# Transposing the probabilities of two attention units together in a three-layer transformer kernel

## The chip, the cores and the metric

The kernel runs on one core of a Trainium2 chip. What counts is the device time of one execution in microseconds (us). The engines are TensorE (PE in the profile; its weight loads are PEld), VectorE (DVE), ScalarE (ACT), GpSimd (POOL) and SyncE (SP), each with its own stream of instructions. They wait for one another by semaphores.

## The reference, cut to what matters

A sequence of 256 tokens of width 1024 goes through an attention layer with two kinds of attention (a windowed one with grouped keys and a sink, here A; a neighbourhood one, here B), an MLP, a retention layer, a second MLP, and then a hybrid layer with three attentions: M (causal), D (causal, over the 256 best keys by an index score) and X (over a memory). All in float32. What the change touches is the softmax in the middle of A, B, M and D:

```python
s = jnp.einsum('bqhd,brkhd->bhqrk', qr, kr).astype(jnp.float32) * scale
s = jnp.where(col_valid[:, None, :], s + bias, -jnp.inf)
p = jax.nn.softmax(s.reshape(B, B_HEADS, GRID_W, kh * GRID_W), axis=-1)
...
return jnp.einsum('bhqrk,brkhd->bqhd', p, vr)
```

## The kernel before

All products with weights are done as three matmuls of split numbers: a weight half tile (128x1024) is copied to `whi` by ScalarE (L969) and the rest, raw minus `whi`, goes to `wlo` on VectorE (L1433). TensorE then streams matmuls over these halves (L415 to L417, L504, L469 to L472). The halves are prepared four or five ahead of TensorE.

Each attention has 8 units of two heads and one block of 128 queries. The units are spread over steps `s`, and each step also holds one half tile of the next projection (`n_half`, `t_half`), so that TensorE has a stream of projection matmuls between two pieces of attention. The sequence "AB" runs A's 8 units and then B's (16 units, 18 steps and one more), "M" and "D" have 8 units each. Every engine has its own program that walks through the same steps, and its order is the order in the code; nothing reorders it later. For unit i the chain is:

- TensorE: `att_scores` (L596), both units of a pair in the even step
- VectorE: `att_scored` (scale and bias, L1545 for A, L1556 otherwise), `att_peaked` (row maxima, L1565 or L1570)
- ScalarE: `att_exp` (L1052), two activations with their sums
- VectorE: `att_summed` (reciprocal, L1585)
- ScalarE: `att_scaled` (L1062), two activations
- TensorE: `att_transposed` (L608), four 128x128 transposes, two where only 128 keys count
- `att_copied`: out of PSUM, on VectorE for an even unit (L1580) and on ScalarE for an odd one (L1074)
- TensorE: `att_values` (L628), both units of a pair, four steps after the scores of the even one

PSUM has 8 banks, `ps0` to `ps7`. `take` in the program of TensorE draws the next bank from a ring and waits until the engine that reads the previous contents is done; `give` puts a bank back as soon as its matmuls are issued:

```python
b = ring.popleft()
if b in held:
    w.wait_ge(*at("free", held[b]))
held[b] = name
```

So which bank a tile gets, and whose reading it waits for, follows from the order of all `take` and `give` calls. Beside the attention, some steps have work of their own: in step 3 of AB ScalarE squares the kb projection (`hn_squares`, L987) and VectorE sums these squares (`hn_sums`, L1457); VectorE applies rotary factors with `roped` (L1662, L1664), which frees the two banks of a projection and, for Dk, may start only when TensorE has transposed the same half of Dq (`rp_transposed`, L578).

## Time and profile before

| | |
|---|---|
| Median of 3 runs | 984.32 us (984.25 to 984.86) |
| The profiled execution | 984.95 us, its span 983.1 us |
| TensorE busy | 973.8 us, 99% of the span |
| VectorE, ScalarE, GpSimd busy | 687.2, 536.1 and 154.8 us |
| Share of TensorE in the chain that ended last | 95% |
| Granted clock over the span | 0.999 |
| AB, M and D, from first scores to last values | about 39 to 117, 753 to 791 and 809 to 848 us |

Read it from the busiest engine. TensorE has work nearly all the time, and the profile's chain of work that ended last is almost wholly its own; idle time of another engine costs nothing by itself.

### The profile page before, as it was taken

How to read it: one execution, taken by the hardware profiler on the slowest of the kernel's cores; microseconds unless marked ns; L12 is line 12 of the kernel's file. 1: busy time of each engine (PE TensorE's matmuls, PEld its weight loads, DVE VectorE, ACT ScalarE, POOL GpSimd, SP SyncE). 2: the span in 40 equal slices, each digit the busy share in tenths (PEclk: the TensorE clock that was granted, in tenths of full speed). 3: DMA queues.
4: the chain of work that ended last, by engine and by line, in shares of the span. 5: the costliest groups of instructions: out<-in, count | busy, mean ns of one | idle time of the engine just before them, and what ended most of it. 6: DMA issues, size and time to landing. Idle time of an engine off the chain costs nothing.

```text
span 983.1 us, 14468 instructions
## 1 busy us (share of the span) xinstructions
PE 973.8 (99%) x5608; PEld 838.5 (85%) x5608; DVE 687.2 (70%) x1036; ACT 536.1 (55%) x900; POOL 154.8 (16%) x193
## 2 busy tenths in 40 slices
PE   9999999999999999999999999999999999999997
PEld 7788788888888888888888888888887789999995
DVE  6797766766666667786567566657678997667674
ACT  6678755444556553454455455444546756655452
POOL 2732017920001002310010000000550100000001
PEclk9999999999999999999999999999999999999999
DMA  9875645575564654445547655664644454545531
GB/s 339 294 184 191 194 145 180 192 222 180 172 203 153 216 200 140 139 147 177 195 146 220 206 172 176 202 220 142 215 142 155 133 171 130 170 131 167 177 129 43
DMA packets 110307, 174.76 MB, mean 178 GB/s; under 512 B 4256, under 2 KB 72992, under 8 KB 110240
## 3 DMA queue, kind: packets, MB, share of 16 engines
q1 hardware_dynamic: 109664, 173.27, 54.0%
q8 instruction: 45, 0.74, 0.3%
q10 hardware_dynamic: 576, 0.57, 0.2%
q14 instruction: 22, 0.18, 0.1%
HBM read 172.78 MB, written 1.05 MB: 177 GB/s over the span
## 4 chain that ended last, share of the span: by engine, by line
PE 95%; ACT 1%; POOL 1%; DMA 1%; DVE 1%; issue 0%; SPq 0%; POOLq 0%; ACTq 0%; DVEq 0%
PE ps L504 24%; PE ps L472 15%; PE ps L415 12%; PE ps L417 12%; PE ps L416 12%; PE ps L470 9%; PE ps L469 2%; PE ps L596 2%; PE ps L608 2%; PE ps L628 1%; DMA raw<-in_w_in_e 1%; PE ps L556 1%; ACT whi L969 0%; PE ps L578 0%; PE ps L646 0%
## 5 line engine op out<-in xcount | busy, mean ns | idle before, releaser
L1433 DVE TENSOR_TENSOR wlo<-raw,whi 128x1024 fp32r<-128x1024 f32 x313 | 376.2, 1239 | 25.1 <-ACT whi L969 12.0
L969 ACT ACTIVATE whi<-raw 128x1024 fp32r<-128x1024 f32 x313 | 315.7, 1048 | 41.9 <-PE ps L504 26.0
L472 PE MATMUL ps<-hT,whi 128*128 128x512 f32 x644 | 229.7, 396 | 0.0
L470 PE MATMUL ps<-hT,wlo 128*128 128x256 f32 x736 | 190.3, 279 | 0.0
L470 PEld LDWEIGHTS ps<-hT,wlo 128*128 128x128 f32 x736 | 138.8, 189 | 7.6
L472 PEld LDWEIGHTS ps<-hT,whi 128*128 128x128 f32 x644 | 120.9, 188 | 25.0
L415 PE MATMUL ps<-whi,hT 128*128 128x512 f32 (+1 forms) x312 | 122.6, 393 | 0.1
L417 PE MATMUL ps<-whi,hT 128*128 128x512 f32 (+1 forms) x312 | 120.1, 385 | 0.0
L416 PE MATMUL ps<-wlo,hT 128*128 128x512 f32 (+1 forms) x312 | 119.9, 384 | 0.0
L1773 DVE TENSOR_TENSOR arena<-ps,arena 128x256 f32<-128x256 f32 x80 | 33.4, 422 | 101.1 <-ACT arena L1182 101.0
L504 PE MATMUL ps<-whi,urh 128*128 128x512 f32 x328 | 101.5, 390 | 0.0
L504 PE MATMUL ps<-wlo,urh 128*128 128x512 f32 x328 | 101.3, 389 | 0.0
L504 PE MATMUL ps<-whi,url 128*128 128x512 f32 x328 | 101.3, 389 | 0.0
L1182 ACT ACTIVATE arena<-ps 128x256 f32<-128x256 f32 x80 | 30.2, 385 | 129.5 <-PE ps L472 129.5
L504 PEld LDWEIGHTS ps<-wlo,urh 128*128 128x128 f32 x328 | 61.6, 188 | 12.9
L504 PEld LDWEIGHTS ps<-whi,url 128*128 128x128 f32 x328 | 61.6, 188 | 12.8
L504 PEld LDWEIGHTS ps<-whi,urh 128*128 128x128 f32 x328 | 61.4, 188 | 11.6
L417 PEld LDWEIGHTS ps<-whi,hT 128*128 128x128 f32 x312 | 58.6, 188 | 11.9
L415 PEld LDWEIGHTS ps<-whi,hT 128*128 128x128 f32 x312 | 58.7, 188 | 11.8 <-ACT whi L969 0.5
L416 PEld LDWEIGHTS ps<-wlo,hT 128*128 128x128 f32 x312 | 58.7, 188 | 10.5
L415 PE MATMUL ps<-hT,whi 128*128 128x256 f32 (+1 forms) x232 | 66.8, 288 | 0.0
L416 PE MATMUL ps<-hT,whi 128*128 128x256 f32 (+1 forms) x232 | 65.6, 283 | 0.0
(216 smaller groups left out, 1495.3 us busy)
## 6 DMA issues: line engine op xcount, KB each, us to landing
raw<-in_w SPq DMA_DIRECT2D x64, 1024.0 KB, 5.9
raw<-in_w_in SPq DMA_DIRECT2D x34, 1024.0 KB, 5.2
raw<-in_w_in_o SPq DMA_DIRECT2D x24, 1024.0 KB, 5.3
raw<-in_w_out_o SPq DMA_DIRECT2D x8, 1024.0 KB, 5.0
raw<-in_w_in_e SPq DMA_DIRECT2D x7, 1024.0 KB, 11.1
raw<-in_w_mem SPq DMA_DIRECT2D x4, 1024.0 KB, 10.7
raw<-in_w_out_e SPq DMA_DIRECT2D x4, 1024.0 KB, 5.0
raw<-in_w_out SPq DMA_DIRECT2D x4, 1024.0 KB, 4.9
```

Of the source, the lines that this page charges most:

```text
L415: e.matmul(o, a[0], b[0], start=start, stop=False)
L416: e.matmul(o, a[0], b[1], start=False, stop=False)
L417: return e.matmul(o, a[1], b[0], start=False, stop=stop)
L469: e.matmul(o, h[:, k, :], both, start=True, stop=False)
L470: mm = e.matmul(o[:, 0:256], l[:, k, :], hT[0][:, k, :], start=False, stop=False)
L472: mm = e.matmul(o, h[:, k, :], both, start=False, stop=k == 7)
L504: mm = e.matmul(bank("acc", stage, 2 * tb + i), x[p], t[p % 2][:, 0, 512 * i:512 * i + 512], start=start and p == 0, stop=stop and p == 2)
L596: mm = e.matmul(b[:, j * 256:j * 256 + nk], q_of(h, qb), k_of(h, nk), start=True, stop=True)
L969: e.activation(split_half(i)[0], raw_half(i), ACT.Copy).then_inc(*up("hi", ("hi", i)))
L1182: e.activation(dst, bank("mm", label, m)[:, 256:512], ACT.Copy).then_inc(*up("aev", ("lc", label, m)))
L1433: e.tensor_tensor(l, raw_half(i), h.bitcast(F32), ALU.subtract).then_inc(*up("lo", ("lo", i)))
L1773: e.tensor_tensor(d, bank("mm", label, m)[:, 0:256], d, ALU.add).then_inc(*up("dev", ("t", label, m), ("free", ("mm", label, m))))
```

## The change

In TensorE's program the transposes of an odd unit no longer stand in the odd step, between two pieces of projection, but in the even step, directly behind those of the even unit. The other two programs are ordered for it: VectorE does both maxima of a pair (`att_scored`, `att_peaked`, twice) at the head of the even step, and copies the even unit's transposed probabilities after them instead of before; ScalarE does in the odd step first the exponentials and then both scalings (they used to stand one before the exponentials and one behind the weights), and copies the odd unit's transposed probabilities in the even step. No instruction is added or removed. X is left as it is.

```diff
--- before.py
+++ after.py
@@ -657,8 +657,9 @@
                 if s % 2 == 0 and s < n:
                     att_scores(*SEQ[key][s])
                     att_scores(*SEQ[key][s + 1])
-                if 0 <= s - 2 < n:
+                if s % 2 == 0 and 0 <= s - 2 < n:
                     att_transposed(*SEQ[key][s - 2])
+                    att_transposed(*SEQ[key][s - 1])
 
             def index_scores(u):
                 qb, hs = IX8[u]
@@ -1076,23 +1077,19 @@
 
             def att_step(key, s):
                 n = len(SEQ[key])
-                if 0 <= s - 2 < n:
-                    att_copied(*SEQ[key][s - 2])
+                if s < n:
+                    att_exp(*SEQ[key][s])
+                if key == "AB" and s == 3:
+                    hn_stored("qb")
                 if key == "AB" and s == 7:
                     v_stored("vb", 0, 512, bvv[:, 1, :], "E")
                 if s % 2 and s < n:
                     att_scaled(*SEQ[key][s - 1])
+                    att_scaled(*SEQ[key][s])
+                if s % 2 == 0 and 0 <= s - 2 < n:
+                    att_copied(*SEQ[key][s - 1])
                 if key == "AB" and s in (8, 9):
                     row_squares("mem", osb, osb, [(S["m"], 16), (S["m"], 16)], (s - 8,))
-                if key == "AB" and s == 3:
-                    hn_stored("qb")
-                if s < n:
-                    att_exp(*SEQ[key][s])
-
-            def att_ends(key, s):
-
-                if s % 2 and s < len(SEQ[key]):
-                    att_scaled(*SEQ[key][s])
 
             def gate_low(label, c):
 
@@ -1171,7 +1168,6 @@
                     v_stored("xv", 0, 512, xv[:, 1, :], "mem")
                 if s in (10, 14):
                     oe_high((10, 14).index(s) + 1)
-                att_ends("AB", s)
             used(("oe", 1), 1)
             oe_high(3)
             used(("oe", 3), 1)
@@ -1324,7 +1320,6 @@
                     used(("Dq", "Dk")[s // 4], s % 4)
                 else:
                     used("Dv", s - 8)
-                att_ends("M", s)
                 if s == 7:
                     y_high(0, 0)
             y_high(0, 1)
@@ -1357,8 +1352,6 @@
                     used(("xq", s // 2), s % 2)
                 else:
                     merge_half(0, s - 4)
-                if s < 10:
-                    att_ends("D", s)
                 if s in (7, 11):
                     y_high(1, s // 11)
             for s in range(16):
@@ -1586,14 +1579,13 @@
 
             def att_step(key, s):
                 n = len(SEQ[key])
-                if 0 <= s - 2 < n:
+                if s % 2 == 0 and s < n:
+                    att_scored(*SEQ[key][s])
+                    att_peaked(*SEQ[key][s])
+                    att_scored(*SEQ[key][s + 1])
+                    att_peaked(*SEQ[key][s + 1])
+                if s % 2 == 0 and 0 <= s - 2 < n:
                     att_copied(*SEQ[key][s - 2])
-                if s < n:
-                    if s % 2 == 0:
-                        att_scored(*SEQ[key][s])
-                    att_peaked(*SEQ[key][s])
-                    if s % 2 == 0:
-                        att_scored(*SEQ[key][s + 1])
 
             def att_ends(key, s):
                 if s < len(SEQ[key]):
@@ -1735,16 +1727,16 @@
                 if s == 7:
                     v_stored("vb", bvv[:, 0, :], "E")
                 att_step("AB", s)
+                weights_to(first_half["kb"] + LO_ROW[s])
+                att_ends("AB", s)
                 if s == 1:
                     hn_scaled("qb")
+                if s == 3:
+                    hn_sums("kb")
+                if s == 5:
+                    hn_scaled("kb")
                 if s in (4, 5, 6):
                     memory_low(range(3 * s - 12, min(3 * s - 9, 8)))
-                weights_to(first_half["kb"] + LO_ROW[s])
-                if s == 5:
-                    hn_scaled("kb")
-                att_ends("AB", s)
-                if s == 3:
-                    hn_sums("kb")
                 if s == 14:
                     v_stored("xv", xv[:, 0, :], "mem")
                 if s in (8, 10, 14):
```


The first place is TensorE in step 4 of AB and the start of step 5 (`ps3` and `ps4` take the scores of units 4 and 5). Before, where "..." stands for the matmuls of half a vb tile:

```order
L596 MATMUL ps3<-arena 128x256 [waits s_aev]
L596 MATMUL ps3<-arena 128x256
L596 MATMUL ps4<-arena 128x256 [waits s_aev]
L596 MATMUL ps4<-arena 128x256
L608 MATMUL ps5<-cst,arena 128x128 x4
L415 MATMUL ps0<-whi3,hT 128x512 [waits s_lo,s_hi]
...
L417 MATMUL ps1<-whi3,hT 128x512
L608 MATMUL ps3<-cst,arena 128x128 [waits s_aev,s_dev]
L608 MATMUL ps3<-cst,arena 128x128 x3
L415 MATMUL ps0<-whi4,hT 128x512 [waits s_lo,s_hi]
```


After:

```order
L596 MATMUL ps3<-arena 128x256 x2
L596 MATMUL ps4<-arena 128x256 [waits s_aev]
L596 MATMUL ps4<-arena 128x256
L608 MATMUL ps5<-cst,arena 128x128 [waits s_aev]
L608 MATMUL ps5<-cst,arena 128x128 x3
L608 MATMUL ps3<-cst,arena 128x128 [waits s_aev,s_dev]
L608 MATMUL ps3<-cst,arena 128x128 x3
L415 MATMUL ps0<-whi3,hT 128x512 [waits s_lo,s_hi]
```


The four transposes of unit 3 have moved up by a half tile of matmuls. They write bank `ps3` in both, but this bank now holds scores that were made four rows earlier, and the row waits for VectorE (`s_dev`) to have read them.

The second place is TensorE in step 8 of M, from the values of units 4 and 5 to the first matmuls of the Dv projection. Before:

```order
L628 MATMUL ps4<-arena 64x128 [waits s_aev,s_dev]
L628 MATMUL ps4<-arena 64x128 x3
L608 MATMUL ps2<-cst,arena 128x128 [waits s_aev,s_dev]
L608 MATMUL ps2<-cst,arena 128x128 x3
L578 MATMUL ps3<-cst,arena 128x128 [waits s_po]
L578 MATMUL ps3<-cst,arena 128x128 x3
L578 MATMUL ps0<-cst,arena 128x128 [waits s_po]
L578 MATMUL ps0<-cst,arena 128x128 x3
L415 MATMUL ps7<-whi0,hT 128x512 [waits s_lo,s_hi]
```


After:

```order
L628 MATMUL ps4<-arena 64x128 [waits s_aev,s_dev]
L628 MATMUL ps4<-arena 64x128 x3
L608 MATMUL ps7<-cst,arena 128x128 [waits s_aev,s_dev]
L608 MATMUL ps7<-cst,arena 128x128 x3
L608 MATMUL ps3<-cst,arena 128x128 [waits s_aev]
L608 MATMUL ps3<-cst,arena 128x128 x3
L578 MATMUL ps6<-cst,arena 128x128 [waits s_po]
L578 MATMUL ps6<-cst,arena 128x128 x3
L578 MATMUL ps5<-cst,arena 128x128 [waits s_po]
L578 MATMUL ps5<-cst,arena 128x128 x3
L415 MATMUL ps1<-whi0,hT 128x512 [waits s_lo,s_hi,s_dev]
```


With the transposes of unit 7 ahead of those of Dq (L578), one more bank has been taken when the Dv projection takes its two, and its first matmul now also waits for VectorE (`s_dev`). The bank is that of Dk's first half, which `roped` frees.

The third place is ScalarE in steps 2 and 3 of AB: exponentials of a unit are two L1052 rows (L1053 after), scalings two L1062 rows (L1063), the weight copy L969 (L970), the copy of unit 1 L1074 (L1075), the stored qb L994 (L995), the squares of kb L987 (L988). Before:

```order
L1052 ACTIVATE arena,stat<-arena,stat 128x257 [waits s_dst]
L1052 ACTIVATE arena,stat<-arena,stat 128x257
L969 ACTIVATE whi<-raw 128x1024 [waits s_wd]
L1074 ACTIVATE arena<-ps 128x512 [waits s_tp]
L1062 ACTIVATE arena<-arena,stat 128x256 [waits s_dst]
L1062 ACTIVATE arena<-arena,stat 128x256
L994 ACTIVATE arena<-ps,gain 128x4x128 x2
L1052 ACTIVATE arena,stat<-arena,stat 128x257 [waits s_dst]
L1052 ACTIVATE arena,stat<-arena,stat 128x257
L987 ACTIVATE arena<-ps 128x512 [waits s_mm] x2
L1062 ACTIVATE arena<-arena,stat 128x256 [waits s_dst]
```


After:

```order
L1053 ACTIVATE arena,stat<-arena,stat 128x257 [waits s_dst]
L1053 ACTIVATE arena,stat<-arena,stat 128x257
L1075 ACTIVATE arena<-ps 128x512 [waits s_tp]
L970 ACTIVATE whi<-raw 128x1024 [waits s_wd]
L1053 ACTIVATE arena,stat<-arena,stat 128x257 [waits s_dst]
L1053 ACTIVATE arena,stat<-arena,stat 128x257
L995 ACTIVATE arena<-ps,gain 128x4x128 [waits s_tp] x2
L1063 ACTIVATE arena<-arena,stat 128x256 [waits s_dst]
L1063 ACTIVATE arena<-arena,stat 128x256
L1063 ACTIVATE arena<-arena,stat 128x256 [waits s_dst]
L1063 ACTIVATE arena<-arena,stat 128x256
L988 ACTIVATE arena<-ps 128x512 [waits s_mm] x2
```


Both scalings of the pair now stand directly ahead of the squares of kb; before, one of them stood behind these.

## Rows read from the trace of the kernel before

**Rows 1.** The page's busy time of TensorE and its granted clock by slices.
```profile
PE 973.8 (99%) x5608; PEld 838.5 (85%) x5608; DVE 687.2 (70%) x1036; ACT 536.1 (55%) x900; POOL 154.8 (16%) x193
...
PEclk9999999999999999999999999999999999999999
```

**Rows 2.** The waits of TensorE, longest first: the first of four rows.
```profile
PE ps L700 <- DVE arena L1709: 1.2, 1, 1.2
```

**Rows 3.** Timeline of TensorE: streams of matmuls and transposes between them.
```profile
43.20 0.39 PE L415 MATMUL ps<-whi,hT 128*128 128x512 f32 x1
...
45.69 0.39 PE L417 MATMUL ps<-whi,hT 128*128 128x512 f32 x1
...
50.34 1.03 PE L568 MATMUL ps<-cst,arena 128*128 128x128 f32 x8
51.21 0.60 PE L608 MATMUL ps<-cst,arena 128*128 128x128 f32 x4
...
59.61 0.39 PE L417 MATMUL ps<-whi,hT 128*128 128x512 f32 x1
...
60.20 0.48 PE L415 MATMUL ps<-whi,hT 128*128 128x512 f32 x1
...
62.83 0.39 PE L417 MATMUL ps<-whi,hT 128*128 128x512 f32 x1
```

**Rows 4.** Timeline around step 4 of AB: TensorE, ScalarE, VectorE.
```profile
56.58 0.66 PE L608 MATMUL ps<-cst,arena 128*128 128x128 f32 x4
...
50.63 0.51 ACT L1052 ACTIVATE arena<-arena,stat 128x257 f32<-128x257 f32 x1 [2.08 <-DVE stat L1567]
...
55.99 1.06 ACT L987 ACTIVATE arena<-ps 128x512 f32<-128x512 f32 x2
...
47.78 0.69 DVE L1580 COPY arena<-ps 128x512 f32<-128x512 f32 x1 [0.18 <-PE ps L608]
48.38 0.40 DVE L1543 COPY arena<-lgt 128x2 f32<-128x2 f32 x1
...
56.60 1.28 DVE L1457 TENSOR_REDUCE stat<-arena 128x8 f32<-128x512 f32 x2 [0.31 <-ACT arena L987]
...
58.46 0.75 DVE L1545 SCALAR_TENSOR_TENSOR arena<-cst,ps 128x256 f32<-128x256 f32 x2
```

**Rows 5.** Timeline around step 8 of D: TensorE, ScalarE, VectorE.
```profile
839.76 0.66 PE L608 MATMUL ps<-cst,arena 128*128 128x128 f32 x4
...
838.05 0.36 ACT L1074 ACTIVATE arena<-ps 128x256 f32<-128x256 f32 x1
838.32 0.90 ACT L1062 ACTIVATE arena<-arena,stat 128x256 f32<-128x256 f32 x2
839.12 0.50 ACT L1052 ACTIVATE arena<-arena,stat 128x256 f32<-128x256 f32 x1
...
840.10 1.05 ACT L969 ACTIVATE whi<-raw 128x1024 fp32r<-128x1024 f32 x1
```

**Rows 6.** Timeline around step 2 of M: TensorE, ScalarE, VectorE.
```profile
759.91 0.44 PE L608 MATMUL ps<-cst,arena 128*128 128x128 f32 x2
...
760.52 0.68 ACT L1062 ACTIVATE arena<-arena,stat 128x128 f32<-128x128 f32 x2
...
759.80 0.16 DVE L1585 RECIPROCAL stat<-stat 128x2 f32<-128x2 f32 x1
```

**Rows 7.** Timeline around step 8 of M: TensorE, VectorE.
```profile
783.06 1.04 PE L578 MATMUL ps<-cst,arena 128*128 128x128 f32 x8
783.85 0.48 PE L415 MATMUL ps<-whi,hT 128*128 128x512 f32 x1
...
783.76 0.75 DVE L1662 SCALAR_TENSOR_TENSOR arena<-ps,stat,cst 128x512 f32<-128x512 f32 x1 [0.84 <-PE ps L578]
784.43 0.87 DVE L1664 SCALAR_TENSOR_TENSOR arena<-ps,stat,cst 128x256 f32<-128x256 f32 x2
```

**Rows 8.** Busy time by engine in one stretch (PE, PEld, DVE, ACT, POOL; clock; DMA).
```profile
750.00:800.00 50.00, 50.00 (x295) 39.93 (x294) 47.05 (x107) 33.09 (x77) 5.20 (x4) 1.00 0.47 148
```

## The prediction

> **What bounds the kernel now.** First the page's busy times and clock: TensorE is busy for 973.8 us, 99% of the span, at the full granted clock of 2.4 GHz in all 40 slices [rows 1]. Then the waits of TensorE: the longest is 1.2 us at the very start, and no row names a wait at the attention's transposes [rows 2]. So the kernel is as long as TensorE's stream. A change can gain only what it takes out of that stream, and every wait that it puts into it counts in full, because no other engine's lateness is now in the way to hide it. I therefore read the timeline next: what a piece of transposes costs the stream, and, for each piece that moves up, when the other engines have its input and its bank ready.
>
> **What it may gain.** Sixteen pieces (the odd units of AB, M and D) leave the middle of projection streams. A lone piece of four costs this: from the last matmul before it to the first behind it 59.61 to 60.20, 0.59 us, in place of one interval of the stream, which is 0.23 (eleven intervals from 43.20 to 45.69). Behind it the eleven intervals from 60.20 to 62.83 take 2.63 instead of 2.49, 0.14 more [rows 3]. That makes 0.59 - 0.23 + 0.14 = 0.50 us. In a longer piece, eight transposes take 50.34 to 51.21, 0.87, so four more cost 0.44 [rows 3]. A merge saves about 0.06. Two of the sixteen stand behind other transposes already (one of them at 51.21 [rows 3]) and save nothing, and in streams of narrower matmuls the tail of 0.14 may be missing. Bounds 0 and 16 x 0.06 = 1.0; I take 0.5.
>
> **What it adds: waits.** The transposes of an odd unit now come a step earlier, one stream of half a tile. I follow each pair through VectorE and ScalarE in their new order, with the durations of the rows. Five places matter. Everything before them on each engine is the same work.
>
> *Step 4 of AB, unit 3.* These transposes write the bank into which the scores of unit 4 went moments before, so they must wait until VectorE has read those scores. VectorE reads them behind the sums for kb, these behind ScalarE's squares, and ScalarE now scales both units ahead of the squares. Before, from the exponentials of unit 2 at 50.63 to the squares at 55.99 ScalarE worked 5.36 us without a gap [rows 4]. The same work stands there now, plus one scaling, 0.80 (838.32 to 839.12 [rows 5]). The exponentials start earlier, since VectorE no longer waits 0.18 for a transpose and copies (0.60, 47.78 to 48.38) ahead of scoring unit 2: 0.78, and up to 1.2 if the 0.40 of the tiny copy at 48.38 is a disturbance that does not recur [rows 4]. I take 0.9. The squares start at 50.63 - 0.9 + 5.36 + 0.8 = 55.9. Before, VectorE was through with the scores 59.21 - 55.99 = 3.22 after the squares started (58.46 + 0.75) [rows 4]; now 0.60 less, since the copy stands behind. The bank is free at 55.9 + 2.6 = 58.5. TensorE is there at about 57.1, half a microsecond behind 56.58 [rows 4]. With 0.1 for the weight load, 1.5 us; 1.2 to 1.8.
>
> *Step 2 of M, unit 1.* The reciprocal for unit 1 is made at 759.80 and takes 0.16; what stands ahead of it on VectorE is the same, only the maxima have changed places, and the maxima directly behind their scores wait some 0.1 for them. The scaling takes 0.68 and was of no hurry at 760.52 [rows 6]. Directly behind the reciprocal it ends at about 760.75. TensorE has transposed unit 0 from 759.91 and wants unit 1 at 760.1 to 760.2 [rows 6]. 0.7 us; 0.5 to 0.9.
>
> *Step 8 of M, the banks of Dv.* With unit 7's transposes ahead, the Dv projection draws the bank of Dk's first half. VectorE frees that with `roped`, which starts only once TensorE has transposed the first half of Dq in this same step. This is a round trip that no other engine's speed can shorten: Dq's transposes start at 783.06, `roped` runs from 783.76 to 785.30 (784.43 + 0.87), 2.24 behind them, and TensorE went on with Dv at 783.85, 0.79 behind them [rows 7]. With 0.15 for the load of the first weights the gap is 2.24 + 0.15 - 0.79 = 1.6 us; 1.4 to 1.8. Before, only unit 7's transposes in step 9 needed that bank, and the half tile in between hid it.
>
> *Step 8 of D, units 6 and 7.* ScalarE scales unit 6 until 839.12, where unit 7's exponentials follow until 840.10 [rows 5]. They now go first (0.98), while the copy (838.05 to 838.32, 0.27) leaves this place: unit 6 is ready at 839.12 + 0.98 - 0.27 = 839.8, or 0.2 earlier if VectorE's earlier start in step 6 reaches ScalarE, and unit 7 another 0.8 later, at 840.4 to 840.6. TensorE wants unit 6 at 839.76 and unit 7 about 0.5 behind [rows 5]. 0.4 us; 0.2 to 0.6.
>
> *The other pairs.* The same count leaves all of them in time. Some are close (unit 1 of A, unit 7 of M, the last pair of B). Together 0 to 0.5; I take 0.1.
>
> Costed at nothing: the copies out of PSUM, which move by a step on ScalarE and behind the scores on VectorE. Their reader is `att_values` two steps later, so two half tiles of stream hide them; without this cover each would cost TensorE its 0.3 to 0.6. ScalarE's weight copies in the odd steps now stand behind both scalings, but they are four halves ahead of their use. SyncE's loads wait only for these, and GpSimd's work does not move.
>
> **The sum.** 1.5 + 0.7 + 1.6 + 0.4 + 0.1 - 0.5 = 3.8 us. TensorE never makes a wait up, since nothing behind it waits for anything else. The profiled execution took 984.95, so it would take 988.75; the median of the runs is 0.63 lower, hence 988.1 us, 0.39% more. With all low ends (1.2 + 0.5 + 1.4 + 0.2 - 1.0 = 2.3) it is 986.6, with all high ones (1.8 + 0.9 + 1.8 + 0.6 + 0.5 = 5.6) 989.9. Some 0.2%, 2 us, is what a measurement of this kernel can tell from no change.
>
> **A rule against it.** All 40 slices show the full clock, and TensorE has hardly stood still in any [rows 1]. The three largest waits are the first such gaps in the middle of the kernel. The Trainium skill, on its page "TensorE: Matmul & The Clock Gate", section "A second HAM failure mode: psum-queue depth-cycling", says that small idle gaps between groups of matmuls, made by the cycling through PSUM banks, let the clock swing between its two levels. What that would do here is the last rival.
>
> **Rivals.**
>
> *The waits are absorbed and nothing is seen.* The step-8 round trip alone leaves 1.6 - 0.5 = 1.1 us, 985.4. For that, the bank in step 4 and unit 1 of M must be ready in time. Against it, each is late by more than half a microsecond in rows that the change leaves alone. For it, my replay joins many rows, and VectorE could run through small instructions faster. It stays within 0.2% if less than 2 us is left of 3.8. Chance 0.10.
>
> *Faster: a merged piece costs far less than its transposes do singly.* If the sixteen pieces came free behind the even ones, the stream would shorten by 16 x 0.50 = 8 us, and with the waits of 4.3 the time would be 980.6. It decides from (4.3 + 2.0) / 16 = 0.39 us a piece. Eight in a row at 0.87 speak against it: 0.11 each, no less than in a lone piece [rows 3]. Chance 0.02.
>
> *Slower still: VectorE does not catch up in M.* From 750 to 800 us it is busy for 47.05 of 50 us [rows 8]; after the round trip its low halves of weights could come late for the stream, and each such wait would cost about what that one costs, 1.6. One or two: 989.7 to 991.3. Against it, a wait of TensorE gives VectorE time too. Chance 0.06.
>
> *The clock falls behind the waits.* At 1.2 GHz the stream of 2.63 us behind a gap [rows 3] would take twice that; one such stretch behind each of the three largest waits adds 3 x 2.6 = 8 us, 996. Against it, the clock holds through the start and its wait of 1.2 us [rows 1, 2]. Chance 0.03.
>
> **How the numbers follow.** My forecast has 0.79. Faster by over 0.2% is the second rival and a remainder, 0.03; within 0.2% the first, 0.10; slower the forecast and the last two, 0.87. The range reaches a little below the low ends, towards the first rival, and up to the high ends, into the third: 986.4 to 989.9.
>
> **What would show it.** The waits of TensorE should now have rows for the transposes (on ScalarE's scaling, L1063), for the transposes of unit 3 at about 57.1 (1.5 us, on VectorE's scoring), and for the first Dv matmul in step 8 of M (1.6 us, on `roped`). TensorE's busy time itself should hardly change, and the streams between the pieces should keep their 0.23. Three waits in these places with other sizes mean that a size was off. If they are missing, the reading of the banks was wrong; if they are there and the span is not longer, so was the statement that TensorE's stream alone sets the end.

## The result, and the profile after

The changed kernel took 989.84 us, the median of 4 runs (989.22 to 990.95); 4 runs of the kernel before on the same chip took 984.59 us (984.25 to 985.12). The ratio is 1.0049, with a 95% interval of 1.0037 to 1.0062. The profiled execution took 990.95 us, its span 989.1. The forecast was 988.1 us in a range of 986.4 to 989.9.

The page of the changed kernel, busy times and granted clock, as in [rows 1]:

```profile
PE 974.6 (99%) x5608; PEld 838.5 (85%) x5608; DVE 688.1 (70%) x1036; ACT 536.4 (54%) x900; POOL 154.0 (16%) x193
...
PEclk9999999999999999999999999999999999999999
```

TensorE's busy time is up by 0.8 us only, the span by 6.0. Almost all of the loss is standing time. The granted clock is 1.00 from 10 to 987 us, as it was from 10 to 981 us before. (The digits alone can't show that: a slice is 25 us long, and 9 stands for 90% or more.) TensorE's waits in the changed kernel, all six rows (total, times, longest), to be read beside [rows 2]:

```profile
PE ps L688 <- ACT hT L1133: 2.0, 2, 1.7
PE ps L608 <- ACT arena L1063: 1.7, 4, 0.6
PE ps L415 <- DVE arena L1656: 1.3, 1, 1.3
PE ps L701 <- DVE arena L1701: 1.2, 1, 1.2
PE ps L608 <- DVE arena L1538: 1.1, 1, 1.1
PE ps L568 <- DVE arena L1462: 0.2, 1, 0.2
```

The second, third and fifth rows are new, and they are the three kinds of wait that were forecast: transposes that wait for ScalarE's scaling, the first matmul of Dv that waits for `roped`, and unit 3's transposes that wait for VectorE to read the scores in their bank. The first row is the start, below. The timeline of TensorE shows each (the figure in brackets is the idle time just before the row and what ended it):

```profile
59.69 0.66 PE L608 MATMUL ps<-cst,arena 128*128 128x128 f32 x4 [1.12 <-DVE arena L1538]
...
763.58 0.41 PE L608 MATMUL ps<-cst,arena 128*128 128x128 f32 x2 [0.61 <-ACT arena L1063]
...
786.92 0.66 PE L608 MATMUL ps<-cst,arena 128*128 128x128 f32 x4 [0.35 <-ACT arena L1063]
787.41 1.04 PE L578 MATMUL ps<-cst,arena 128*128 128x128 f32 x8
789.71 0.50 PE L415 MATMUL ps<-whi,hT 128*128 128x512 f32 x1 [1.26 <-DVE arena L1656]
...
845.81 0.63 PE L608 MATMUL ps<-cst,arena 128*128 128x128 f32 x4 [0.58 <-ACT arena L1063]
846.61 0.63 PE L608 MATMUL ps<-cst,arena 128*128 128x128 f32 x4 [0.17 <-ACT arena L1063]
```

Idle time in these rows leaves out the modelled end of the matmul before it, so it understates a wait. I price a wait from the starts of neighbouring matmuls instead: the start of one minus the start of the one before, less the usual distance at this place (0.109 within transposes; 0.203 from L628 to L608 in D; 0.03 from a transpose to L415).

| Place in the changed kernel | start to start, us | usual | wait | forecast |
|---|---|---|---|---|
| step 2 of AB, unit 1 | 0.377 | 0.109 | 0.27 | in the 0.1 for other pairs |
| step 4 of AB, unit 3 | 1.391 | 0.109 | 1.28 | 1.5 |
| step 16 of AB, last unit of B | 0.192 | 0.109 | 0.08 | in the 0.1 for other pairs |
| step 2 of M, unit 1 | 0.887 | 0.109 | 0.78 | 0.7 |
| step 8 of M, unit 7 | 0.623 | 0.109 | 0.51 | in the 0.1 for other pairs |
| step 8 of M, first Dv matmul | 1.530 | 0.03 | 1.50 | 1.6 |
| step 8 of D, unit 6 | 0.857 | 0.203 | 0.65 | 0.4 for both |
| step 8 of D, unit 7 | 0.443 | 0.109 | 0.33 | |

That is 5.40 us, of which the small wait of B matters only for the balance below; I call the other seven the waits. Is it all? TensorE executes the same 4712 matmuls with weights, in the same order, in both kernels, so I subtract the start of each in the kernel before from its start here. The difference at 44 us, before the first moved transpose has an effect, is what the start did; what it grows by afterwards is the change:

| grows, counted from 44 us, us | AB | M | D | to the end |
|---|---|---|---|---|
| changed kernel | 1.57 | 2.77 | 0.59 | 4.93 |
| changed kernel, a second profile | 1.55 | 2.75 | 0.59 | 4.89 |

The seven waits make 5.32, and the sum at the end is 4.93. The largest item of the difference is a wait of the kernel before that is gone, 0.38. It stood at the last values of D, which waited for ScalarE's copy of unit 7 (L1074 there); in the changed kernel TensorE comes later and the copy stands in a better place. In the profile of before:

```profile
846.32 0.28 PE L417 MATMUL ps<-urh,wlo 128*128 128x256 f32 x1
846.91 1.09 PE L628 MATMUL ps<-arena 128*64 128x128 f32 x16 [0.31 <-ACT arena L1074]
```

From 846.32 to 846.91 is 0.59 us; the changed kernel takes 0.21 for this step. Three smaller items all but cancel one another. The wait of B adds 0.08. The second matmul behind a wait mostly starts 0.02 to 0.06 later than usual too, which makes 0.24 for all of them. And the merged transposes give back some 0.3 (see "One sequence alone").

The profiled execution of the changed kernel also began 1.06 us late, which is no part of the change: TensorE waited 1.7 us for the first inputs (first row of its waits above) where the kernel before waited 0.7 in its profile. In the 12 profiles of the experiments below this start lies between 0.71 us earlier and 1.13 later than in the profile of before, and the changed kernel alone had 1.06 later in one profile and 0.71 earlier in another. The time of every profiled execution is that of before plus its start and its growth, within 0.05 us. For the runs without a trace it isn't shown, but they spread by about as much. So I read small differences from the trace, counted from 44 us.

### The profile page after: what moved, and what is told of

The parts are those of the page before. It is cut to its first block and busy times, and to the rows that moved or that the text cites. A ratio compares the mean times of both kernels' runs of the same rounds, so it can differ in the third digit from the quotient of the medians.

```text
span 989.1 us, 14475 instructions
## 1 busy us (share of the span) xinstructions
PE 974.6 (99%) x5608; PEld 838.5 (85%) x5608; DVE 688.1 (70%) x1036; ACT 536.4 (54%) x900; POOL 154.0 (16%) x193
## 5 line engine op out<-in xcount | busy, mean ns | idle before, releaser
L970 ACT ACTIVATE whi<-raw 128x1024 fp32r<-128x1024 f32 x313 | 315.2, 1047 | 41.6 <-PE ps L504 26.0
L415 PE MATMUL ps<-whi,hT 128*128 128x512 f32 (+1 forms) x312 | 122.1, 391 | 1.4 <-DVE arena L1656 1.3
L415 PEld LDWEIGHTS ps<-whi,hT 128*128 128x128 f32 x312 | 58.7, 188 | 13.3 <-DVE arena L1656 1.5
L417 PEld LDWEIGHTS ps<-whi,hT 128*128 128x128 f32 x312 | 58.6, 188 | 11.9
L415 PE MATMUL ps<-hT,whi 128*128 128x256 f32 (+1 forms) x232 | 66.6, 287 | 0.0
```

What stands on the lines that cost most here:

```text
L415: e.matmul(o, a[0], b[0], start=start, stop=False)
L417: return e.matmul(o, a[1], b[0], start=False, stop=stop)
L970: e.activation(split_half(i)[0], raw_half(i), ACT.Copy).then_inc(*up("hi", ("hi", i)))
```

## The experiments

In every one I give the time, and the growth from 44 us to the end as above. The experiments stand in three groups, each with runs of the kernel before beside it: 985.36 us (22 runs) for the sequences alone and the first run on the orders; 985.11 (21) for the second run on the orders, TensorE alone, the banks and the reciprocals; 985.05 (21) for the rest.

### One sequence alone

Each of the three has the change in one of the sequences AB, M and D, on all three engines, and is as before in the others.

```diff
-                if 0 <= s - 2 < n:
+                if key in MERGED:
+                    if s % 2 == 0 and 0 <= s - 2 < n:
+                        att_transposed(*SEQ[key][s - 2])
+                        att_transposed(*SEQ[key][s - 1])
+                elif 0 <= s - 2 < n:
                     att_transposed(*SEQ[key][s - 2])
```

> The change in the sequence AB alone; M and D as before. Theory of the waits (each wait of TensorE counts in full, and they add up by sequence): from the trace of the changed kernel, AB holds the bank wait at unit 3 (1.28 us more than a normal start) and 0.2 us at step 2, so +1.3 to +1.6 us against before. Rival (the cost lies in the move of the transposes as such, spread evenly over the 16 pieces): half of the 4.9 us, +2.4 us.

> The change in M alone. Theory of the waits: unit 1 (0.78), unit 7 (0.51), the bank of Dk in step 8 (1.50): +2.7 to +2.9 us against before. Rival (spread evenly over the pieces): a quarter of 4.9, +1.2 us.

> The change in D alone. Theory of the waits: 0.98 us at the transposes of units 6 and 7, less 0.4 us that TensorE waited before for the copy of unit 7 ahead of the last values: +0.5 us against before. Rival (spread evenly): +1.2 us.

| | time, us | ratio (95%) | growth |
|---|---|---|---|
| AB | 986.69 | 1.0015 (1.0006 to 1.0024) | 1.55 |
| M | 988.50 | 1.0031 (1.0020 to 1.0043) | 2.79 |
| D | 985.21 | 0.9999 (0.9990 to 1.0008) | 0.60 |

The three add up to 4.94, what the whole change costs. So the parts are independent, and a wait in one sequence doesn't shift another's.

The same growth shows what merging saves. At each pair it rises by what the odd unit's transposes cost in their new place, and falls when TensorE passes their old place. In AB alone, behind unit 3, the four pairs up to 100 us rise by 0.44 (four transposes at 0.109) and fall by 0.44, back to 1.55: nothing is saved. Their odd pieces stood in streams of 256-column matmuls or behind other transposes. Where they stood in streams of 512 columns, the fall is larger than the rise: unit 3 falls by 0.49, the last two pairs of B by 0.52 and 0.49, and the four of M by 0.03 to 0.06 more than their transposes cost. In D it is nothing again. In all that is some 0.3 of the 0.5 in the forecast. In AB the 0.14 that the last two pairs save is used up by the 0.14 that the wait of B costs with the matmul behind it, so that the growth ends at 1.55 as if nothing had happened.

### The order on VectorE and ScalarE, with TensorE as before

Here all transposes stay where they were, and the other two engines have their new order. As the odd unit's transposes come in the odd step again, its copy on ScalarE belongs there; I put it at the end of that step.

```diff
                 if s % 2 and s < n:
                     att_scaled(*SEQ[key][s - 1])
                     att_scaled(*SEQ[key][s])
-                if s % 2 == 0 and 0 <= s - 2 < n:
-                    att_copied(*SEQ[key][s - 1])
+                if s % 2 and 0 <= s - 2 < n:
+                    att_copied(*SEQ[key][s - 2])
```

> TensorE as before, with the odd unit's transposes in the odd step; VectorE and ScalarE in the new order, but ScalarE copies the odd unit's transposed probabilities in the odd step, behind both scalings. Theory of the waits: the cost is all in TensorE's new place for the transposes, so none of the waits at L608 and L415 is there and the time is that of before, within 0.1% (984 to 985.2 us). Rival (the new order on VectorE and ScalarE is itself the loss): +2 us or more.

It took 1007.1 us (1006.34 to 1010.81), 1.0232 of before (1.0216 to 1.0248), with a growth of 21.6. My expectation was wrong. The waits say where it went:

```profile
PE ps L629 <- ACT arena L1079: 19.6, 12, 2.3
```

Twelve times the values waited for ScalarE's copy, up to 2.3 us. The copy stands behind two exponentials and four scalings there, and its reader comes one stream later. I had costed the copies at nothing in the forecast because two half tiles cover them. That was right for the change, where the reader comes two steps behind the transposes; here it comes one step behind them, and the copy stands last. The waits are not the whole of it. The clock fell once, behind the longest wait of AB:

```profile
78.50 1.45 PE L629 MATMUL ps<-arena 128*64 128x128 f32 x16 [2.28 <-ACT arena L1079]
79.88 2.09 PE L597 MATMUL ps<-arena 64*128 64x256 f32 x8
81.90 0.93 PE L609 MATMUL ps<-cst,arena 128*128 128x128 f32 x4
...
79.10:82.50 3.40, 3.40 (x21) 2.26 (x17) 0.51 (x1) 0.68 (x1) 0.00 (x0) 0.50 1.03 417
```

The last row is the stretch from 79.10 to 82.50 us with its granted clock, 0.50, that is 1.2 GHz; the transposes in it start 0.213 apart instead of 0.109. The growth over this place is 3.92, of which 2.35 is the wait, so the slow clock cost about 1.6 us. Waits of the same length in M and D (2.28 and 2.23) have no such stretch behind them. The page's digits are all 9 in this run too.

To see the orders themselves, I ran it again with the copy at the head of the odd step:

```diff
+                if s % 2 and 0 <= s - 2 < n:
+                    att_copied(*SEQ[key][s - 2])
                 if s < n:
                     att_exp(*SEQ[key][s])
```

> TensorE as in the kernel before; VectorE and ScalarE in the new order, but ScalarE copies the values of the odd unit's predecessor at the head of the odd step and not behind the scalings. If the copy's place behind both scalings was the whole cost of the new orders with the old transposes (19.6 us of waits on it), the time is that of the kernel before within 0.1%. If the new orders of maxima, exponentials and scalings cost by themselves, some 5 us or more stay.

985.91 us, ratio 1.0008 (0.9999 to 1.0017), growth 0.94: nearly what before takes, as the first theory said. The 20 us were the copy's place, by its waits and the stretch of slow clock. But 0.94 us is only just within the 0.1% that I had allowed, and the trace gives it two places:

```profile
71.85 0.28 PE L418 MATMUL ps<-urh,wlo 128*128 128x256 f32 x1
72.28 0.39 PE L416 MATMUL ps<-urh,whi 128*128 128x256 f32 x1
...
841.13 0.63 PE L609 MATMUL ps<-cst,arena 128*128 128x128 f32 x4 [0.84 <-ACT arena L1067]
```

At 72 us a matmul of the stream starts 0.31 late. At 841 the transposes of unit 6 of D wait 0.9 for its scaling although they stand in their old place: this wait is made by the new orders of VectorE and ScalarE, not by the pairing on TensorE. (Unit 7, in its old place one step later, doesn't wait.) It is won back in part by the wait for the last copy, which is gone here too.

### TensorE alone

The reverse: pairs of transposes on TensorE, the other engines as before.

> Only TensorE changed: transposes of both units in the even step, VectorE and ScalarE as in the kernel before. The odd unit is then scaled at the very end of its step, behind a pass over weights, and TensorE should wait for it at nearly every even step by 0.5 to 2 us, besides the two bank waits: 8 to 16 us above the kernel before. If the orders of VectorE and ScalarE do not matter for it, it takes what the whole change takes, 5 us above.

997.71 us (997.19 to 997.75), 1.0124 of before (1.0110 to 1.0137), growth 12.75, in the middle of the expected range.

```profile
PE ps L609 <- ACT arena L1067: 8.5, 7, 1.9
PE ps L609 <- DVE arena L1565: 1.5, 1, 1.5
PE ps L416 <- DVE arena L1693: 1.3, 1, 1.3
```

Seven times the odd unit was not scaled yet, and not at nearly every even step, as I had expected. So the reordering of ScalarE and VectorE is worth 8 of these 12.75 us. The other two rows, 1.5 and 1.3, are the two bank waits. They are there with either order, since TensorE's order alone decides who draws which bank. How long unit 3 waits also depends on when the others come to it.

### The two bank waits

If unit 3 waits because VectorE reads the scores behind the sums for kb, ScalarE's squares must come earlier; if Dv waits for the round trip from Dq's transposes to `roped`, these transposes must come ahead of the attention's. In this run both are so, and the rest is the changed kernel:

```diff
                 if key == "AB" and s == 3:
                     hn_stored("qb")
+                    hn_squares("kb")
...
+                if s == 8:
+                    rp_transposed("Dq")
                 att_step("M", s)
-                if s == 8:
-                    rp_transposed("Dq")
```

(ScalarE's `rp_stored("Dq")` moves ahead of its own step in the same way.)

> The changed kernel with two bank holders released earlier: ScalarE squares kb ahead of the two scalings in step 3 of AB, and in step 8 of M the first half of Dq is transposed (TensorE) and stored (ScalarE) ahead of the attention's step. If the two bank waits are what I take them for (VectorE's late reading of the scores of unit 4; the round trip from Dq's transposes to roped), the wait at unit 3's transposes falls from 1.3 us by 1.1 and that at the first Dv matmul from 1.5 us by 1.3: about 2.4 us less than the changed kernel, some 2.3 to 2.5 above the kernel before. If the waits have another cause, or only move to the next user of a bank, the time stays within 0.5 us of the changed kernel's, some 5 above before.

987.60 us (985.88 to 988.05), 1.0019 of before (1.0011 to 1.0028), growth 2.03, that is 2.9 less than the changed kernel. TensorE at both places:

```profile
57.47 0.66 PE L608 MATMUL ps<-cst,arena 128*128 128x128 f32 x4
58.44 0.65 PE L608 MATMUL ps<-cst,arena 128*128 128x128 f32 x4 [0.32 <-DVE arena L1537]
...
784.63 0.38 PE L578 MATMUL ps<-cst,arena 128*128 128x128 f32 x2
784.95 0.66 PE L628 MATMUL ps<-arena 128*64 128x128 f32 x8
785.53 1.09 PE L608 MATMUL ps<-cst,arena 128*128 128x128 f32 x8
786.38 0.47 PE L415 MATMUL ps<-whi,hT 128*128 128x512 f32 x1
```

The Dv wait of 1.50 is gone entirely, and with it the 0.51 at unit 7 of M, because its transposes now come 0.9 us later in the program: that is the part of the gain beyond the 2.4 that I expected. Both causes are confirmed. The 0.8 at unit 3 is less than the 1.1 that I expected there: 0.48 is left (0.589 from start to start) where I expected 0.2. VectorE stood idle for 0.70 us until the scores were written and was through with them 0.05 before the transposes started. So what is left is the bare round trip of a bank that one step both fills with scores and asks for again.

### The reciprocals first

VectorE's reciprocals (`att_ends`) ahead of the weights in odd steps; otherwise the changed kernel. In M:

```diff
+                if s < 10 and s % 2:
+                    att_ends("M", s)
                 if s < 12:
                     used(("Dq", "Dk", "Dv")[s // 4], s % 4)
...
-                if s < 10:
+                if s < 10 and s % 2 == 0:
                     att_ends("M", s)
```

> The changed kernel with VectorE's reciprocals of the sums ahead of the weights' low halves in the odd steps of AB, M and D. If the waits at the transposes of units 1 and 7 of M come from reciprocals that stand behind a pass over weights, they shrink by about 0.6 and 0.5 us: 1.1 us less than the changed kernel. The waits at units 6 and 7 of D, which ScalarE's own row of work sets, stay at about 1.0. If ScalarE's work is what is late in M too, nothing changes (within 0.2 us).

989.14 us (988.56 to 989.62), 1.0038 of before (1.0025 to 1.0050), growth 4.10, 0.8 less than the changed kernel. The wait at M's unit 7 is gone and that at unit 1 is down from 0.78 to 0.14; units 6 and 7 of D keep 0.65 and 0.34, as expected. In AB the same move did harm: unit 3's bank wait grew from 1.28 to 1.75, though unit 1's 0.27 went. VectorE's passes, not ScalarE's, made the two places in M late: the reciprocal stood behind a pass over weights of 1.2 us. The gain is smaller than the two waits (1.15) for a new wait in M, 0.29, which the next run but one shows too, and for AB, where the growth ends at 1.64 instead of 1.57 (unit 3's longer wait less the waits at unit 1 and at the last unit of B).

### The tanh late

```diff
-                if r == 2:
+                if r == 2 and (i, g) != (0, 0):
                     gate(i, g, 0)
...
                 if s < 10:
                     att_step("D", s)
+                if s == 7:
+                    gate(0, 0, 0)
```

> The changed kernel, with ScalarE's first tanh of the merge (and its wait of 0.9 us for VectorE) moved from step 6 of D to behind the scalings of step 7. If the waits at units 6 and 7 of D (0.98 us together) come from the row of work that ScalarE has to do between the exponentials of unit 6 and the scalings, both are gone: 1.0 us less than the changed kernel. If VectorE's reciprocals are what is late there, less than 0.3 us goes.

989.78 us (989.34 to 989.99), 1.0046 of before (1.0034 to 1.0059), growth 4.38, 0.5 less than the changed kernel. Unit 6's wait of 0.65 is gone; unit 7's is 0.43 (0.543 from start to start) instead of 0.33. Half of the theory held. What ScalarE did ahead of the scalings made unit 6 late, and behind that stands VectorE, whose reciprocal of unit 7 is made at 843.75, behind weights (ScalarE stands 0.89 us for it before it scales unit 7):

```profile
842.61 1.22 DVE L1428 TENSOR_TENSOR wlo<-raw,whi 128x1024 fp32r<-128x1024 f32 x1
843.75 0.16 DVE L1580 RECIPROCAL stat<-stat 128x2 f32<-128x2 f32 x1
```

There is no run with both the late tanh and the reciprocals first in D, so the cause of unit 7's wait is read from rows and not tested.

### All of it mended

This has the banks' edits, the reciprocals first in M, and the late tanh.

> The changed kernel with all of it mended: kb squared first and Dq's first half transposed first (as in the run on the banks), reciprocals first in the odd steps of M alone, and the tanh late. The transposes still come in pairs. By the waits left in the earlier runs (0.48 at unit 3, 0.27 at unit 1 of A) it takes 4.89 - 0.80 - 1.50 - 0.51 - 0.78 - 0.98 = 0.3 us more than the kernel before, no difference that can be measured. If the pairs of transposes cost something by themselves, or the waits move elsewhere, 2 us or more stay; if pairs save what I had thought (0.5), it is 0.2 us under before.

986.48 us (985.70 to 987.71), 1.0016 of before (1.0007 to 1.0024), growth 1.51, where I had expected 0.3. Every wait that I had taken away is gone or has the size that the runs above left it. But two places in M wait now that do not in the changed kernel (the first of them did in the run with the reciprocals first). TensorE, the second row of each pair being the first matmul behind the transposes:

```profile
768.71 1.09 PE L608 MATMUL ps<-cst,arena 128*128 128x128 f32 x8
769.83 0.50 PE L415 MATMUL ps<-whi,hT 128*128 128x512 f32 x1
...
785.18 1.09 PE L608 MATMUL ps<-cst,arena 128*128 128x128 f32 x8
786.32 0.50 PE L415 MATMUL ps<-whi,hT 128*128 128x512 f32 x1
```

From the row of eight transposes to the stream is 1.12 and 1.14 us here, and 0.85 in the run on the banks (785.53 to 786.38). The extra 0.27 and 0.29 are new waits, for `roped`, which frees the bank. It ends at 769.78 (768.91 + 0.87) and at 786.26 (785.39 + 0.87), 0.05 us before each stream begins:

```profile
768.91 0.87 DVE L1657 SCALAR_TENSOR_TENSOR arena<-ps,stat,cst 128x256 f32<-128x256 f32 x2
...
785.39 0.87 DVE L1657 SCALAR_TENSOR_TENSOR arena<-ps,stat,cst 128x256 f32<-128x256 f32 x2
```

The run on the banks has nearly the same growth ahead of M (0.76, here 0.79) and no wait at either place, so it tells the causes apart. Counted from each run's start, TensorE wants the second bank 0.3 us earlier here, and `roped` ends 0.08 later: this wait was mostly hidden behind the one at unit 1. The first is another case. `roped` ends there 0.4 us later than in the run on the banks, and that is more than the wait. The delay begins with the reciprocals. Put ahead of the weights, the one of unit 1 stops VectorE until ScalarE has made the sums, and behind it VectorE works almost without a break up to `roped` and can't make this up:

```profile
768.55 0.86 DVE L1655 SCALAR_TENSOR_TENSOR arena<-ps,stat,cst 128x256 f32<-128x256 f32 x2
...
760.38 0.17 DVE L1579 RECIPROCAL stat<-stat 128x2 f32<-128x2 f32 x1 [0.16 <-ACT arena L1053]
```

(The first row is the run on the banks, whose start is 0.04 us later than this one's; the second is this run.)

The sum by places: 0.27 and 0.48 in A; 0.14, 0.27 and 0.29 in M; 0.43 in D less the 0.38 of the last copy. That is 1.50 of 1.51; the gain of the merged pieces and the small costs that this sum leaves out cancel here as well.

### The transposes of A's first two pairs apart

As the run before, but units 1 and 3 of A are transposed in steps 3 and 5, as in the kernel before, and ScalarE squares kb behind both scalings, as in the changed kernel (the expectation's "new place" is wrong for this kernel).

```diff
                     att_transposed(*SEQ[key][s - 2])
-                    att_transposed(*SEQ[key][s - 1])
+                    if key != "AB" or s not in (2, 4):
+                        att_transposed(*SEQ[key][s - 1])
+                if key == "AB" and s in (3, 5):
+                    att_transposed(*SEQ[key][s - 2])
```

> As the run before it, but units 1 and 3 of A keep their transposes in steps 3 and 5 as in the kernel before, so the bank that unit 4's scores hold is not asked for at once; kb is squared in its new place. No wait at transposes should be left, and the one for ScalarE's copy of unit 7 in D (0.3 to 0.4 us) is gone: 0.4 us less than the kernel before by the trace, too little for the times to tell. If a wait of 0.5 us or more is left at a transpose, my account of the banks is not whole.

987.61 us (986.71 to 988.03), 1.0023 of before (1.0014 to 1.0032), growth 2.12. It should have been the fastest and is slower than the run beside it. The two waits in A are gone, and the growth is 0.03 at 64.5 us. Then:

```profile
66.10 0.63 PE L608 MATMUL ps<-cst,arena 128*128 128x128 f32 x4 [0.44 <-ACT arena L1066]
...
72.94 0.38 PE L415 MATMUL ps<-urh,whi 128*128 128x256 f32 x1 [0.41 <-DVE url L1438]
```

Unit 5 waits 0.60 for its scaling, and the stream 0.57 for a low half of the memory (0.692 from start to start, usual 0.120), both made by VectorE; some 0.15 more are slower intervals behind the second. In the changed kernel TensorE was 1.5 us late by then and never saw either: the waits at units 1 and 3 had hidden them. The growth over AB is 1.40, almost the 1.57 that it was with the two waits. By the sign that I had set, a wait of 0.5 us or more at a transpose, my account was not whole: it had the banks, which don't wait here, but not what their waits had covered. The late matmul at 72 us in the run on the orders alone (0.31) stands at the same place: the change puts the memory's low halves behind the weights and the reciprocals on VectorE.

### The changed kernel once more

> The changed kernel once more, on the same chip as the three beside it and with more runs: 1.0050 of before, 4.9 us more, with the same six waits at the same places (1.28, 0.27, 0.78, 0.51, 1.50, 0.98 us within 0.1); only the first inputs' wait, which differed by 1.1 us in its profiled execution, may be another.

990.22 us (989.13 to 990.38) beside 985.05, 1.0049 (1.0035 to 1.0063), growth 4.89. All seven waits have the same sizes within 0.01. The start came 0.71 us earlier than in the profile of before, where the other profile had it 1.06 later.

## Why the prediction was right, and where its sizes were off

The forecast was slower by 3.8 us: 4.3 of waits at named places, less a gain of 0.5. The growth is 4.9: 5.4 of waits at these places and three that it had named as close, less what else changed. The mechanism was right. That the time fell into the range was in part luck: 989.84 lies 0.06 us under its upper end, and the second timing of the same kernel, 990.22 (where before took 985.05), lies over it. By its own steps:

- **What bounds the kernel.** TensorE's busy time moved by 0.8 us and its waits by 5; every wait counted in full. That the clock was full in all 40 slices said less than I took from it, since a 9 stands for 90% or more. The runs with one sequence each add up to the whole, 1.55 + 2.79 + 0.60. Right.
- **The gain, 0.5.** It was some 0.3. The prices were right: a lone piece in a 512-column stream falls out with 0.49 and costs 0.44 behind another. But only seven pieces stood in such streams by themselves, and those of M gave 0.03 to 0.06 each. In the growth even the 0.3 can't be seen. The second matmul behind each wait is late too, 0.24 in all, for which I had counted nothing.
- **Unit 3 of A, 1.5.** It was 1.28. The bank came free when I said: VectorE ends its reads at 58.90 + 0.74 = 59.64, which less the late start of 1.06 is 58.6, forecast 58.5. TensorE came 0.27 later than forecast, since unit 1's wait had held it up. The forecast added waits that here share an interval. Its allowances of 0.1 here and 0.15 at Dv for a weight load came from no row: from the end of VectorE's reading to the next matmul it is 0.05 us at both.
- **Unit 1 of M, 0.7.** 0.78. Right; the run with the reciprocals first shows the cause.
- **Dv's bank, 1.6.** 1.50. Right, and the run on the banks takes it away.
- **Units 6 and 7 of D, 0.4.** 0.98. ScalarE's scalings begin at 844.78 in the changed kernel. TensorE is 5.40 us behind the kernel before at this place, so that is 839.4 on the old clock, and unit 6 is ready at 840.2 instead of 839.8. What the replay missed is ahead of the exponentials of unit 7: the tanh on ScalarE waits for VectorE's L1961, which now stands behind both units' maxima. It starts at 842.03 - 5.40 = 836.6, where before it started at 836.3. I had let VectorE's new order only bring work forward. The run with the late tanh shows this for unit 6; for unit 7 it left 0.43, which rows put down to the reciprocal. ScalarE in the changed kernel:

```profile
840.78 0.36 ACT L1075 ACTIVATE arena<-ps 128x256 f32<-128x256 f32 x1
842.03 0.91 ACT L1345 ACTIVATE arena<-arena,lgt 128x256 f32<-128x256 f32 x2 [0.88 <-DVE arena L1961]
842.84 1.04 ACT L970 ACTIVATE whi<-raw 128x1024 fp32r<-128x1024 f32 x1
843.79 0.49 ACT L1053 ACTIVATE arena<-arena,stat 128x256 f32<-128x256 f32 x1
...
844.78 1.69 ACT L1063 ACTIVATE arena<-arena,stat 128x256 f32<-128x256 f32 x4
```

- **What D gives back, not in the forecast.** 0.38, the wait for the last copy. I had looked for waits that the change makes, and not at the small ones that the kernel before already had.
- **The other pairs, 0.1.** 0.86: unit 7 of M 0.51, unit 1 of A 0.27 and the last unit of B 0.08. All three were named as close, and even the upper bound of 0.5 was too low. Beside D this is the term that was most mis-sized. In M the reciprocal of unit 7 stands behind a pass over weights, as that of unit 1 does, for which I had counted 0.7:

```profile
784.64 1.21 DVE L1426 TENSOR_TENSOR wlo<-raw,whi 128x1024 fp32r<-128x1024 f32 x1
785.77 0.16 DVE L1578 RECIPROCAL stat<-stat 128x2 f32<-128x2 f32 x1
```

So the sum reads 1.28 + 0.78 + 1.50 + 0.98 + 0.86 + 0.24 - 0.38 - 0.33 = 4.93 in place of 3.8. The gain of 0.33 is what is left over in it; added up from the pieces it is some 0.3. Of the rest of the miss, 988.1 against 989.84, the level of these runs is some 0.3 (before took 984.59 there against 984.32). The other 0.3 or so are within what the start does to a median of four.

- **The rivals.** The waits were not absorbed. Merged pieces are not cheap. VectorE does not fall behind in M: from 750 to 800 us its busy time is 46.23 instead of 47.05 [rows 8], and no stream waits for weights.

```profile
750.00:800.00 50.00, 47.78 (x278) 37.71 (x277) 46.23 (x101) 29.89 (x73) 5.16 (x4) 1.00 0.43 134
```

- **The clock.** The same row has a granted clock of 1.00 over the stretch with waits of 0.78, 0.51 and 1.50, and it is 1.00 from 10 to 987 us. The rule from the page "TensorE: Matmul & The Clock Gate" of the Trainium skill, section "A second HAM failure mode: psum-queue depth-cycling", would have given 996 us by my rival. The trace of the changed kernel does not show it for waits of this size and number; as the Trainium skill puts it there, the idle gaps must come frequently enough, with the cycling in each iteration. But the clock can fall in this kernel. With 19.6 us of waits in twelve places, in the first run on the orders, the clock fell to 0.50 for 3.4 us behind one of them.

What stays open: why that one wait had a slow clock behind it and eleven others had not, and whether the savings in the 512-column streams, read from starts of matmuls, hold when nothing else is moved. No run tests either.

## What to carry to other kernels

When one engine is the bound and its stream is moved, look at each moved piece for two things: whether the piece's input is made by then, and whose bank it draws now, since an order of `take` and `give` is part of the change. A wait that the bounding engine has early in the kernel hides waits behind it: removing two of 1.28 and 0.27 us brought out others of 0.60 and 0.57. A mend can also make a wait of its own, as the reciprocals did. So a sum of waits read from one trace is a good forecast of what a change costs, and too hopeful a one of what its removal gives. And before an operation is counted as moved forward, ask what was moved behind it: the order of two maxima delayed the input of ScalarE's tanh, and that the scalings for which TensorE waited. Last, a total of zero can be a gain and a loss of the same size: look at each place where the difference rises and falls before you call a gain absent.

## What the runs showed of the hardware

Four transposes of 128x128 cost TensorE 0.44 us behind others. Alone they cost the same in a stream of 256-column matmuls (units 7, 9 and 11 of AB), and 0.49 to 0.52 in one of 512 columns (units 3, 13 and 15 of AB). After a wait the next matmul started 0.05 us behind the end of VectorE's reading (unit 3 of A, Dv), and the one after it mostly another 0.02 to 0.06 late. The start of the kernel varied by up to 1.8 us between profiled executions (0.71 earlier to 1.13 later than before's), in a wait for the first inputs, and this accounts for what these executions differ by beside their growth. TensorE's granted clock stayed at 1.00 through the waits of up to 1.5 us in the changed kernel. In the run with twelve waits of up to 2.3 us idle it fell once, to 0.50 for 3.4 us, behind one of 2.28, at a cost of about 1.6 us.
